# Forgetting attention: the row-maximum products read rounded copies of queries and keys

## The reference

```python
def forgetting_attention(h, w_in, b_forget, q_gain, k_gain, w_out):
    ...
    q = rmsnorm(q.reshape(B, Lp, ATT_HEADS, ATT_HEAD_DIM), q_gain).transpose(0, 2, 1, 3)
    k = rmsnorm(k.reshape(B, Lp, ATT_HEADS, ATT_HEAD_DIM), k_gain).transpose(0, 2, 1, 3)
    ...
    logf = jax.nn.log_sigmoid(fl.astype(jnp.float32) + b_forget.astype(jnp.float32))
    c = jnp.cumsum(logf, axis=1).transpose(0, 2, 1)
    ...
        s = jnp.einsum('bhqd,bhkd->bhqk', q_i, k).astype(jnp.float32) * scale
        s = s + c_i[..., :, None] - c[:, :, None, :]
        mask = (pos[None, :] <= p_i[:, None]) & (pos[None, :] >= pad)
        p = jax.nn.softmax(jnp.where(mask, s, NEG), axis=-1)
        return jnp.einsum('bhqk,bhkd->bhqd', p.astype(v.dtype), v)
    ...
    o = o * jax.nn.sigmoid(og)
    return (o @ w_out)[:, pad:]
```

## Time and profile before

| | us |
|---|---|
| median of 3 runs | 2736.95 |
| lowest and highest | 2735.82, 2739.54 |
| span of the profiled execution | 2732.2 |
| TensorE busy in it | 2546.3 (93%) |
| VectorE busy | 1369.3 (50%) |
| ScalarE busy | 973.2 (36%) |
| GpSimd busy | 985.7 (36%) |

### The profile page before, as it was taken

One profiled execution on the slowest core, in us unless ns is written; L12 is line 12 of the kernel. 1 busy time (PEld: TensorE's weight loads), 2 busy tenths in 40 slices (PEclk: granted clock), 3 DMA queues, 4 the chain that ended last, 5 costly groups with the idle time before them and its releaser, 6 DMA issues.

```text
span 2732.2 us, 45723 instructions
## 1 busy us (share of the span) xinstructions
PE 2546.3 (93%) x19794; PEld 2286.5 (84%) x19794; DVE 1369.3 (50%) x2057; ACT 973.2 (36%) x1565; POOL 985.7 (36%) x585
## 2 busy tenths in 40 slices
PE   7989978799999999999999999989998979999997
PEld 5877767678888888887999999988988968999997
DVE  4634455462635354444264554466654534727363
ACT  5234344232323444334433332354332224333232
POOL 1743344544444322222434444500002214445444
PEclk9999999999999999999999999999999988999998
DMA  9432120333332221111222332322111012233221
GB/s 248 121 94 63 53 70 24 92 96 97 93 93 87 68 55 47 40 47 40 78 62 85 89 90 85 87 59 70 40 33 36 17 32 59 85 92 87 87 87 60
DMA packets 379927, 201.33 MB, mean 74 GB/s; under 512 B 6464, under 2 KB 377152, under 8 KB 379728
## 3 DMA queue, kind: packets, MB, share of 16 engines
q1 hardware_dynamic: 379728, 198.42, 25.8%
HBM read 196.30 MB, written 2.10 MB: 73 GB/s over the span
## 4 chain that ended last, share of the span: by engine, by line
PE 57%; DVE 22%; ACT 11%; issue 4%; POOL 4%; DMA 1%; POOLq 0%; ACTq 0%; SPq 0%; DVEq 0%
PE ps L645 40%; DVE t_ffy L2829 7%; ACT t_wh L613 5%; DVE t_ffy L2832 2%; ACT t_ffy L2736 2%; DVE t_atq L2628 2%; POOL t_wl L623 1%; PE ps L2436 1%; DVE t_wl L623 1%; DVE t_ffy L2838 1%; PE ps L3061 1%; PE ps L2409 1%; PE ps L2375 1%; PE ps L3080 1%; PE ps L1090 1%
## 5 line engine op out<-in xcount | busy, mean ns | idle before, releaser
L623 POOL TENSOR_TENSOR t_wl<-t_raw,t_wh 128x1024 fp32r<-128x1024 f32 (+2 forms) x268 | 611.1, 2281 | 1030.1 <-ACT t_wh L613 1030.1
L613 ACT ACTIVATE t_wh<-t_raw 128x1024 fp32r<-128x1024 f32 (+2 forms) x323 | 327.7, 1015 | 605.8 <-PE ps L645 562.4
L645 PE MATMUL ps<-t_hh,t_wh 128*128 128x264 f32 (+2 forms) x2048 | 473.4, 310 | 14.4 <-DVE t_dcq L2562 3.6
L645 PE MATMUL ps<-t_hh,t_wl 128*128 128x264 f32 (+2 forms) x2048 | 449.4, 298 | 8.0 <-POOL t_wl L623 4.3
L645 PE MATMUL ps<-t_hl,t_wh 128*128 128x264 f32 (+2 forms) x2048 | 446.0, 299 | 0.0
L645 PEld LDWEIGHTS ps<-t_hh,t_wh 128*128 128x128 f32 x2048 | 323.7, 192 | 36.5 <-issue 17.6
L645 PEld LDWEIGHTS ps<-t_hh,t_wl 128*128 128x128 f32 x2048 | 324.0, 191 | 24.2 <-POOL t_wl L623 6.9
L645 PEld LDWEIGHTS ps<-t_hl,t_wh 128*128 128x128 f32 x2048 | 322.6, 191 | 9.1 <-issue 1.5
L645 PE MATMUL ps<-t_fhh,t_wh 128*128 128x264 f32 (+1 forms) x1040 | 280.9, 324 | 6.5 <-DVE t_fhl L1753 4.9
L645 PE MATMUL ps<-t_fhh,t_wl 128*128 128x264 f32 (+1 forms) x1040 | 281.5, 325 | 4.6 <-POOL t_wl L623 4.5
L2829 DVE SCALAR_TENSOR_TENSOR t_ffy<-t_ffp,t_vec,t_ffy 128x528 f32<-128x528 f32 x88 | 216.8, 2463 | 130.6 <-ACT t_ffy L2736 130.6
(11 more groups left out here) (558 smaller groups left out, 4351.3 us busy)
## 6 DMA issues: line engine op xcount, KB each, us to landing
t_raw<-in_up SPq DMA_DIRECT2D x44, 512.0 KB, 3.8
t_raw<-in_up2a SPq DMA_DIRECT2D x44, 512.0 KB, 3.9
t_raw<-in_up2b SPq DMA_DIRECT2D x44, 512.0 KB, 3.9
t_raw<-in_attn_in SPq DMA_DIRECT2D x33, 512.0 KB, 4.1
t_raw<-in_dn_in SPq DMA_DIRECT2D x33, 512.0 KB, 4.1
t_raw<-in_ada_w SPq DMA_DIRECT2D x32, 512.0 KB, 4.4
t_raw<-in_w_in SPq DMA_DIRECT2D x25, 512.0 KB, 4.4
t_raw<-in_down SPq DMA_DIRECT2D x16, 512.0 KB, 3.8
```

The source lines that it names most:

```text
L613: ac.activation(wh[slot_of[j]][:, 0:kc, :], raw[r % NRAW][:, 0:kc, :], ACT.Copy).then_inc(up("wh_cut", "cut", j), 1)
L623: eng.tensor_tensor(wl[slot_of[j]][:, 0:kc, :], raw[r % NRAW][:, 0:kc, :], wh[slot_of[j]][:, 0:kc, :].bitcast(F), SUB).then_inc(up(name, " ...
L645: ins = pe.matmul(ps[bank_of(j, i)][:, 0:tn], wt[slot][:, k, :], a[:, k, t0:t0 + tn], start=first, stop=last)
```

## The change

Two tiles are added, `kround` and `qround` (`t_akr`, `t_aqr`), 128 by 528 in float32r. Each is set up in the place of tiles that are set up after it (`cT` and the tile of the gate's logarithms), so that no memory is added; the first use of them has to wait for the last use of those. A step `round` is put into the plan just ahead of a pair's first `row_max` item. In it ScalarE copies the pair's queries and keys whole, rounded to float32r, and signals `rounded`. The matmul of `row_max` on queries and keys reads these copies, and waits for `rounded` in place of `normed`. `weights` still reads the float32 tiles, and waits for `normed` itself.

```diff
+        with ExitStack() as st:
+            kround = sbt(st, "akr", [128, L], R)
         cT = sbt(sb_, "cT", [16, L])
...
+        with ExitStack() as st:
+            qround = sbt(st, "aqr", [128, L], R)
         glog = sbt(sb_, "aglog", [128, L])
...
                 if p < 8:
+                    put("round", p)
                     for i in range(6):
                         put("row_max", p, i, banks=2)
...
-                for m in range(2):
-                    w.wait_ge(s.normed, at("normed", "pair_norm", p, m))
+                w.wait_ge(s.rounded, at("rounded", "round", p))
...
-                    pe.matmul(ps[b][0:tn, 0:wide], aq[p % 3][64 * e:64 * e + 64, t0:t0 + tn],
-                              ak[p % 3][64 * e:64 * e + 64, a:a + wide], start=True, stop=False)
+                    pe.matmul(ps[b][0:tn, 0:wide], qround[64 * e:64 * e + 64, t0:t0 + tn],
+                              kround[64 * e:64 * e + 64, a:a + wide], start=True, stop=False)
...
+                for m in range(2):
+                    w.wait_ge(s.normed, at("normed", "pair_norm", p, m))
...
+            def round_(p):
+                for m in range(2):
+                    w.wait_ge(s.normed, at("normed", "pair_norm", p, m))
+                if p == 0:
+                    w.wait_ge(s.turned, at("turned", "split_c"))
+                    w.wait_ge(s.lo_dve, at("lo_dve", "split_c"))
+                else:
+                    w.wait_ge(s.scored, at("scored", "row_max", p - 1, 5))
+                ac.activation(qround[:, :], aq[p % 3][:, :], ACT.Copy)
+                ac.activation(kround[:, :], ak[p % 3][:, :], ACT.Copy).then_inc(up("rounded", "round", p), 1)
```

More of the change, by code:

```diff
@@ L111 @@
     "lev_in lo_dve lo_pool mask_in maxed mm_done mod_mm mod_part mod_set multiplied normed out_d pool_step pool_x "
-    "rel_in rooted roped rstd_a rstd_d scaled scored sin_in sp_done sp_in sp_out spread sq_dve sq_pool "
+    "rel_in rooted roped rstd_a rstd_d scaled scored rounded sin_in sp_done sp_in sp_out spread sq_dve sq_pool "
     "squared step_x summed took_a took_d turned vec_in weighed wh_cut wl_dve wl_pool "
@@ L2032, in program @@
             "pair_norm": "multiplied rooted inverted normed",
-            "values": "turned copied", "row_max": "scored maxed", "turn_max": "turned copied",
+            "values": "turned copied", "round": "rounded", "row_max": "scored maxed", "turn_max": "turned copied",
             "weights": "scored exped", "mixing": "weighed inverted scaled",
@@ L2549, in forget_scalar @@
             return {"cumulated": cumulated, "log_gates": log_gates, "gates_log": gates_log, "att_consts": att_consts,
-                    "split_c": split_c, "pair_sq": pair_sq, "pair_norm": pair_norm, "sig_act": sig_act, "values": values,
+                    "split_c": split_c, "pair_sq": pair_sq, "pair_norm": pair_norm, "round": round_, "sig_act": sig_act, "values": values,
                     "turn_max": turn_max, "weights": weights, "gated": gated}, {
```

## The result

| | before | after |
|---|---|---|
| median, us | 2736.39 | 2766.94 |
| lowest and highest (4 runs each, on one chip) | 2735.19, 2739.54 | 2765.05, 2771.70 |
| after / before, 95% interval | | 1.0112 (1.0100 to 1.0123) |
| span of the profiled execution | 2732.2 | 2763.9 |

A forecast was written before the change was run, and what follows sets the result against it. TensorE was taken to set the time in the attention stretch. Profiled span 2732.2 + waits 27.6 - format 11.5 + lower clock 10.5 = 2758.8 us; with 4.75 us from span to median, 2763.5 us, range 2751 to 2777.

The forecast's parts named there:

- waits of pairs 0, 2, 3, 4: Ahead of item 0, TensorE waits for ScalarE's copies behind table load and sigmoid: 4 x 4.26 us, 17.0 us lost.
- waits of pairs 5, 6: Ahead of item 0, copies stand behind a square, not table load and sigmoid: 2.86 us each, 5.7 us lost.
- pair 1: Copies follow the last exponentials, so TensorE waits only 0.25 us at item 0.
- pair 7: Copies stand behind `t_oh`: 6.00 us wait, less 1.43 us of a VectorE wait that goes away; net 4.6 us.
- format: Float32r in `row_max` products saves 1.60 us a pair, but 0.26 at pair 1: 11.5 us gained.
- lower clock: TensorE runs 3.4 us at clock 0.50 behind each of seven waits, losing 1.5 us each: 10.5 us.
- wait for `t_amx`: TensorE's wait for VectorE's reductions: longer at pair 1, about 3 us, and none at pair 7.
- Rival (b): Lower-clock stretches behind the waits last about twice as long: 2774 us; chance 0.10.
- Rival (a): TensorE's clock doesn't fall after the waits: 2753 us; chance 0.11.
- Rival (c): The float32r format of the `row_max` products saves nothing: 2775 us; chance 0.03.
- Rival (d): ScalarE's copies are done when TensorE gets there, so only the saving is left: 2725.5 us; chance 0.04.
- Rival (e): Waits for the copies of about 1.4 us, at which the clock holds: no change, 2737 us; chance 0.02.

The follow-up runs named there:

- e3: Against after, step `round` of pairs 2 to 7 put right behind the values' copies, ahead of panel rounding, table load and sigmoid; 2747.0 us, 1.0031 of before.
- e5: Against e4, pair 0 has no step `round` and keeps its float32 product and wait for `normed`; 2726.5 us, 0.9964 of before.
- e2: Against after, TensorE multiplies constants during the waits ahead of each pair's first item, except at pair 1; 2755.0 us, 1.0062 of before.
- e1: Against after, `row_max` products read the float32 tiles again, rounded copies still made and waited for; 2782.6 us, 1.0163 of before.
- e4: Against after, step `round` of pairs 2 to 7 put ahead of the values' copies; 2732.7 us, 0.9988 of before.
- e7: Against e5, step `round` of pair 4 put back where the change had it; 2738.2 us, 1.0002 of before.

## Why the prediction was right

The mechanism held in each part, and the median came 3.4 us over the forecast. By its steps (the format as counted at the full clock):

| term | forecast, us | in after, us |
|---|---|---|
| waits of pairs 0, 2, 3, 4 | 4 x 4.26 | 4 x 4.14 |
| waits of pairs 5, 6 | 2 x 2.86 | 2 x 2.72 |
| pair 1 | 0.25 | 0.11 |
| pair 7 | 6.00 - 1.43 | 5.85 - 1.43 |
| waits in all | 27.6 | 26.5 |
| format | -11.5 | -12.1 |
| lower clock | 7 x 1.5 = 10.5 | 42.9 x 0.44 = 19 |
| sum | 26.6 | 33.4 (the stretch: 32.4) |

That the time came so close is in part luck, since one term, the clock, was 8.5 us short. The waits and the format gave 1.7 us of that back. Another 3.4 us came back by what the prediction had not weighed: the stretch is 1.0 us shorter than the terms add up to, the rest of the program is 0.7 us shorter, and the median of after lies 3.0 us over its profiled span, where the prediction added 4.75.

**The waits** were read from where ScalarE and TensorE stood in the trace before, and are right within 4% in all. Each is 0.12 to 0.15 us shorter, since the two copies took 1.16 us and not 1.25, and the first starts before the instruction ahead of it ends. (The 4.06 us in brackets above is 4.14 counted from the moment at which item 0 was due.) The wait for `t_amx` went away at pair 7, as said, and e3 to e5 have it back, at 1.55 to 1.70 us: where item 0 comes in time, VectorE is the one that is late.

**The format.** Items 0 and 1 take 0.93 us where they took 1.18, items 2 and 3 1.65 for 2.48, items 4 and 5 1.01 for 1.61: 1.69 us a pair at the full clock, where 1.60 were forecast. That 1.60, with the 1.34 that items 2, 3 and 4 have in it, was my estimate and no run shows it; what the runs showed in its place is 1.69, and 1.31 for those three items. Pair 1 keeps 0.28 us (item 0 to item 5 is 10.33 us for 10.61) where the same estimate gave 0.26, because item 5 waits for VectorE. That is 7 x 1.69 + 0.28 = 12.1 us. A count on another kernel agrees: e5 gains 6 x 1.69 + 0.28 = 10.4, loses 6.8 x 0.44 = 3.0 to the clock and 0.3 by a longer wait at pair 7 (1.70 us for 1.43), 7.1 in all, and its stretch is 7.5 us shorter than before.

**The clock is the term that was mis-sized:** 19 us, not 10.5. The 10.5 us forecast are 3.4 us at 0.50 behind each of the seven waits of 2.86 us or more. That failed twice. Stretches in after run over 3.4 to 10.2 us, and TensorE is active in them for 4.3, 4.8, 9.4, 5.2, 3.4, 6.8 and 5.5 us behind the seven waits, 39.4 us and not 23.8. In five of the seven the fall begins in the pause itself, where it costs nothing, but those five stretches last 6.8 us or more. And there is an eighth, of 3.4 us, at pair 1. The prediction itself said that the wait for `t_amx` would grow to about 3 us there (it is 2.65) and never priced the clock behind it:

```profile
1019.47 0.45 PE L2379 MATMUL ps<-t_akr,t_aqr 64*128 64x400 f32 x2 [2.65 <-DVE t_amx L2659]
```

The clock fell 2.5 us after the end of this pause. Rival (b), stretches twice as long, named the size (21 us against 10.5) with a chance of 0.10, and is nearer in this term than the forecast; its time, 2774 us, is 7 us over the measured one. Rival (a), the clock holds, is excluded by the traces, and e2 shows what it would have looked like. Rival (c), that the format saves nothing (2775 us), is excluded by e1, 15.7 us over after, and by the item of 400 keys, 0.48 us for 0.95.

**Rival (d),** copies that are done in time, is what e5 builds. Its mechanism was right, and so was the reason against it: nothing in the order of the change brings ScalarE there sooner. (A wait of 2.9 us would have had to shrink by half only to come to 1.4, and not by two thirds as was said; none moved by more than 0.15 us.) That the time it was given, 2725.5 us, lies so near e5's 2726.5 is partly chance: it has the saving of all eight pairs and no fall of the clock, e5 has that of seven pairs and one fall, and its stretch gained 7.5 us and not 11.5.

**Rival (e),** waits of about 1.4 us and no change, is nearly what e3 builds: its waits are 4.1, 0.1 and six of 1.24, 11.6 us or 1.45 a pair. It took 2747 us and not 2737, because the clock fell three times. So the point at which the change neither gains nor loses lies at shorter waits than the prediction's 11.5 / 8, which had no price for the clock in it.

How much of the loss is which: the waits 26.5, the clock 19, the format gives 12 back. e2 shows the clock's part by taking it away (15.5 us in the stretch, with one fall left that is worth 2.9), e1 the format's, and e3 and e4 those of waits and clock together by their place. That the shares add up to 33.4 and the stretch is 32.4 us longer leaves 1 us. The factor 0.44 is that of panel matmuls (1 - 0.245 / 0.44); e2 gave 0.43 over all the work, which would take half of that 1 us away. The rest is open.

## What to carry to other kernels

A step that is added to an engine with plenty of idle time costs nothing or everything by its place in that engine's order: here the same two copies cost 30.6 us behind a table load and a sigmoid, and gained 10 us where they were placed some 6 us sooner, in a wait that was there anyway (with the first pair left out, whose operands come too late for that). Before such a step is put in, look on the timeline for what stands ahead of it at the moment when its reader is due. A new pause of TensorE of 2.6 us or more cost with the clock behind it 1.7 times its length in after (26.5 and 19 us) and twice its length in e7: price it so, and price the pauses that the change makes longer too, not only the new ones.

## What the runs showed of the hardware

- **The clock fell after shorter pauses than I had counted with.** In the attention stretch of all the kernels TensorE's granted clock fell to 0.50 with each of 23 pauses of 2.64 to 5.77 us, and not with most of those of 1.15 to 1.80 us, but it did with two of the fifteen: one of 1.17 us in e3, where four others of 1.17 us left it at 1.00, and one of 1.70 us in e7, where the same pause in e5 left it at 1.00.
- **The same pause did not give the same stretch.** The pause of 2.65 us at pair 1 is followed by 3.4 us at 0.50 in after, 2.5 us later, and in e5 by 6.8 us at once:

```profile
1018.70:1025.40 6.70, 6.70 (x32) 5.08 (x34) 2.51 (x7) 0.00 (x0) 0.00 (x0) 0.50 0.15 47
```

- **Matmuls on constants during a wait kept the clock at 1.00** in e2 and were worth 15.5 us of the stretch and 11.9 us of the median, with the wait itself unchanged.
- **ScalarE's copy of 128x528 from SBUF to SBUF into float32r takes 0.63 us,** 1.16 us for two, and no table load (1.28 us) stood between them and the work around them.
- **In float32r the product of queries and keys has two records where float32 has four,** and an item of 400 keys fell from 0.95 to 0.48 us. How these times divide into weight loads and matmuls was not shown.
